# Keeping the keys of a gated recurrence as logarithms: scaled keys straight from the exponential

## The chip, the cores and the metric

The kernel runs on one core of a Trainium2 chip. The metric is the device time of one execution in microseconds (us). Before the change three runs took 2671.22, 2671.25 and 2673.91 us, with a median of 2671.25 us. The engines are PE (matmul; PEld are its weight loads), DVE (vector), ACT (scalar, with the exponential), POOL (GpSimd) and SP (which issues the transfers).

## The reference, cut to what matters

Two layers of an encoder, over 1024 tokens of one new stream and 16 tokens of each of 8 running streams. The first layer's mixer A is a linear recurrence with a decay for each channel, evaluated in blocks:

```
q, fz, i_in, g, p = split(h @ w_in)
log_f = logaddexp(log(lb), log1p(-lb) + log_sigmoid(fz))    # lb is 0 here: log_sigmoid(fz)
k = (1 - lb) * sigmoid(-fz)
q = silu(q) * 128 ** -0.5
b = cumsum(log_f) in the block
scores[t, s] = sum_k q[t,k] * k[s,k] * exp(b[t,k] - b[s,k])     for s <= t
o = scores @ v + (q * exp(b)) @ S
S = exp(b_last) * S + (k * exp(b_last - b)).T @ v
```

After it come an RMS norm for each head, a gate, mixer B (means over the last 2, 4, 8 and 16 tokens with a small product), the output projection, a gated feed-forward net with a convolution, and then a second layer of another kind. The change touches mixer A alone.

## The kernel before, in words

Activations lie with channels on the 128 partitions and tokens on the free axis: 1152 tokens, nine tiles of 128, of which the last holds the samples. `work` has 24 rows of 1152 tokens (its index is called a slot below): 0 to 3 queries, 4 to 7 keys, 8 to 11 values, 12 to 15 gates, 16 to 19 the pooling input, 20 to 23 the running sums b.

**The projection.** `w_in` is applied unit by unit (20 units of 128 output channels, the order is `UNITS`). Every product is three passes, high and low part of weights and input, so a unit is 72 matmuls of 384 columns. ACT makes the high part of a weight piece (`high`), DVE the low part (`low`), POOL multiplies the piece by the norm's gain before that (`scale_weights`), and DVE takes the result out of the banks (`scaled`, `evict`). Units 0 to 8 (`BESIDE = 9`) run alone. In them ACT and DVE turn the forget inputs into log f and keys (`logf_step`, `logf`, `log_keys`, `key_step`), and DVE's scans make b (`decay`, one row of 1152 tokens for each head).

**The attention beside units 9 to 19.** Tile after tile is worked on between the matmuls of a unit (`beside`; `kk` counts its eight parts of nine matmuls). The sample tile p = 0 goes beside units 9 to 12, and tiles p = 1 to 8 beside units 12 to 19. One tile beside its unit is called turn p here. The scores of a tile are the diagonal (`diagonal`) and seven levels (`level`, four for the samples) of block size b = 64 down to 1: within each block of 2b tokens the second half's queries meet the first half's keys, both scaled by exponentials of b minus its value at the middle. A level goes through these steps, each one instruction:

- DVE `diff(m)`: exponents into `ediff`;
- ACT `exponents(m)`: exp of the query half, exp of minus the key half;
- DVE `scale_queries(m)` into `qsc`, POOL `scale_keys(m)` into `ksc`;
- PE `level(m)`: four matmuls; DVE `take(m)`: the masked result into `sct`.

`ediff`, `qsc` and `ksc` have two buffers each. All order is written out by hand: each engine has its own program, and counting semaphores join them. On DVE step q of a turn (q = 1 to 7) does `scale_queries` of level q and `diff` of the level after the next one, on ACT the exponentials of the level after the next one, and on PE `kk` = q - 1 does level q. F is the number of a turn's first level below.

**What else a turn holds.** PE turns the tile's values (`turn_values`, kk 0), its decayed keys (`turn_keys`, kk 5), sums the squares of an earlier tile's outputs (`head_sums`, kk 1, in `spare`), does pooling products, and ends with `outputs` and `state_update` (kk 7). ACT squares those outputs for `head_sums` (`head_square`) at q = 2, takes the root of the sums (`head_root`) at q = 3, and in turns 7 and 8 makes high parts of mixer B's result (`pool_high`); DVE multiplies by the root (`head_norm`) at q = 4 and makes the low parts (`pool_low`).

POOL waits in `scale_keys(m)` until PE has done level m - 2, because `ksc` has two buffers:

```
pool.wait_ge(ek_ready, keys_scaled(m))
if m >= 2:
    pool.wait_ge(level_mm, m - 1)
```

Of the kernel before, what the change touches and what calls it, by code (L numbers as in the profile page):

```python
# [17 lines left out]
F32 = mybir.dt.float32  # L18
# [67 lines left out]
def build(nc, A, O):  # L86
    ctx = ExitStack()
    with ctx:
# [78 lines left out]
        k_scaled = sem("k_scaled")  # L167
# [3 lines left out]
        diag_in = sem("diag_in")  # L171
        kd_diff = sem("kd_diff")
        kd_exp = sem("kd_exp")
        kd_scaled = sem("kd_scaled")
# [138 lines left out]
        resetm = at("resetm", [P, TOK], F32, E0)  # L313
# [3 lines left out]
        vmb = (stt[:, :, :], work[:, 4:8, SEQ:TOK])  # L317
        hstage = work[0:NS * HIST, 4:8, SEQ:TOK]
        poolw = work[:, 20:24, SEQ:TOK]
        prow = (work[:, 8:12, 0:P], work[:, 20:24, 0:P])  # L320
# [5 lines left out]
        ph = at("ph", [P, HEADS, TOK], F32R, slot(20))  # L326
# [316 lines left out]
        HALF = {True: (64, 32, 16, 8, 4, 2, 1), False: (8, 4, 2, 1)}  # L643
# [7 lines left out]
        def keys_scaled(m):  # L651

            return m + 1 - sum(b == 1 for _, b in LEVELS[:m + 1])
# [4 lines left out]
        def eqd(p):  # L658

            return work[:, 8:12, SEQ:TOK] if p else work[:, 20:24, SEQ:TOK]  # L660
# [4 lines left out]
        def pool_part(r):  # L665

            g, c = ((slice(1, 4), tbs(0)), (slice(1, 4), tbs(1)), (slice(0, 1), slice(0, 2 * TB)),
                    (slice(0, 4), tbs(2)))[r]
            return work[:, 16:20, :][:, g, c], ph[:, g, c], pl[:, g, c]
# [328 lines left out]
        def _(pe):  # L998
# [222 lines left out]
            def turn_keys(p):  # L1221
                pe.wait_ge(kd_scaled, p + 1)
# [4 lines left out]
            def diagonal(p):  # L1227
                for h in range(HEADS):
                    mm = pe.matmul(ps[5][:, h * P:(h + 1) * P], work[:, 4 + h, cols(p)], work[:, h, cols(p)],
                                   start=True, stop=True)  # L1230
                mm.then_inc(diag_mm, 1)

            def level(m):
# [3 lines left out]
                if b > 1:  # L1237
                    pe.wait_ge(k_scaled, keys_scaled(m))
                if m >= 2:
                    pe.wait_ge(level_in, m - 1)  # L1240
                for h in range(HEADS):
                    key = ksc[:, m % 2, h, 0:last] if b > 1 else work[:, 4 + h, cols(p)][:, 0:last]
# [54 lines left out]
            def head_sums(i, bank):  # L1297
                pe.wait_ge(osq_ready, i + 1)
                for h in range(HEADS):
                    mm = pe.matmul(ps[bank][:, h * P:(h + 1) * P], ones[:, :], work[:, 4 + h, cols(NORMS[i])],  # L1300
# [3 lines left out]
            def after_samples(kk):  # L1304

                if kk == 0:
                    pe.wait_ge(acc_free, g0 + 24)
                    pe.wait_ge(k_ready, 2)
# [142 lines left out]
            def abo_half(u, n, h, after=None):  # L1451
# [4 lines left out]
                for k in range(4):  # L1456
# [3 lines left out]
                    for c, (w, r) in enumerate(((wh, rh), (wh, rl), (wl, rh))):  # L1460
                        for tb in range(NTB):
                            mm = pe.matmul(ps[3 * u + tb][:, 0:TB], w[:, n % 2, k * P:(k + 1) * P], r[:, k, tbs(tb)],
# [20 lines left out]
            def abo_unit(n, g, sn, sg):  # L1483

                for h, (rh, rl) in enumerate(((oh, ol), (ph, pl))):
                    pe.wait_ge(w_high_ready, n + h + 1)
                    pe.wait_ge(w_low_ready, n + h + 1)
                    for k in range(4):
                        for c, (w, r) in enumerate(((wh, rh), (wh, rl), (wl, rh))):
                            first, last = h == k == c == 0, h == 1 and k == 3 and c == 2  # L1490
                            for tb in range(NTB):
                                if first:
                                    acc_bank(g + tb, sg + tb)
                                mm = pe.matmul(ps[(sg + tb) % BANKS][:, 0:TB], w[:, (sn + h) % 2, k * P:(k + 1) * P],  # L1494
                                               r[:, k, tbs(tb)], start=first, stop=last)
# [7 lines left out]
            def abo_group(d, tb):  # L1503
# [3 lines left out]
                for h, (rh, rl) in enumerate(((oh, ol), (ph, pl))):  # L1507
# [3 lines left out]
                    for k in range(4):  # L1511
                        if tb == 2 and d == 5 and h == 0 and k == 3:
                            norm_block(0, 1, ssq_e)
                        for c, (w, r) in enumerate(((hi, rh), (hi, rl), (lo, rh))):
                            mm = pe.matmul(ps[(g0 + e) % BANKS][:, 0:TB], w[:, k * P:(k + 1) * P],  # L1515
                                           r[:, k, tbs(tb)], start=h == k == c == 0, stop=h == 1 and k == 3 and c == 2)
# [265 lines left out]
        def _(dve):  # L1782
# [13 lines left out]
            def scaled(dst, bank, tb, tick):  # L1796

                dve.wait_ge(pe_tick, tick)
                dve.tensor_tensor(dst, ps[bank % BANKS][:, 0:TB], rstd[:, tbs(tb)], ALU.mult)\
                    .then_inc(acc_free, 1)  # L1800
# [50 lines left out]
            def first_blocks(j, tb, tick):  # L1851
                dve.wait_ge(rms_ready, tb + 1)
                scaled(work[:, UNITS[j], tbs(tb)], 3 * j + tb, tb, tick)
# [9 lines left out]
            def logf(c):  # L1863
                z, f = work[:, 4 + 2 * c:6 + 2 * c, :], work[:, 20 + 2 * c:22 + 2 * c, :]
# [3 lines left out]
            def log_keys(c):  # L1868
                z, f = work[:, 4 + 2 * c:6 + 2 * c, :], work[:, 20 + 2 * c:22 + 2 * c, :]
                dve.wait_ge(logf_ready, c + 1)  # L1870
                dve.tensor_tensor(z, f, z, ALU.subtract).then_inc(logf_ready, 1)

            def decay(h):
                dve.wait_ge(logf_ready, 3 + h // 2)
                dve.wait_ge(reset_ready, 3)
                dve.tensor_tensor_scan(work[:, 20 + h, :], resetm[:, :], work[:, 20 + h, :], 0.0,
                                       ALU.mult, ALU.add).then_inc(decay_ready, 1)

            for j in range(2, BESIDE):
                if j > 2:  # L1880
                    low(2 * j + 1, 2 * j + 1)
                if j == 6:
                    logf(1)
                    log_keys(0)
# [2008 lines left out]
```

## Time and profile before

| | |
|---|---|
| median of three runs | 2671.25 us |
| the profiled execution | 2671.41 us |
| its span | 2669.7 us |
| PE, PEld busy | 2625.6 us (98%), 2555.8 us (96%) |
| DVE busy | 1845.3 us (69%) |
| ACT busy | 937.5 us (35%) |
| POOL busy | 261.6 us (10%) |
| mean granted clock of PE | 0.999 |

The shares are means over stages that differ. The stage of the change lies in the first sixth of the span: units 0 to 8 run until about 131.5 us, the attention stands beside units 9 to 19 until about 406 us, and the output projection follows. A turn is counted here from one tile's diagonal (line 1229) to the next. Times in the rows are microseconds from the span's start. "Matmuls are pipelined": a PE row's length goes on past the moment at which the next may start, so the distance between starts says what PE had to do.

### The profile page before, as it was taken

To read this page: it belongs to the slowest core of one execution; us is meant where nothing else is said; L and a number is where in the kernel's file an instruction comes from. 1 tells how busy PE (TensorE), PEld (TensorE's weight loads), DVE (VectorE), ACT (ScalarE), POOL (GpSimd) and SP (SyncE) were. 2 spreads that over 40 slices of the span, in tenths; PEclk is the share of its full clock that TensorE was granted. 3 is DMA by queue.
4 is the path that set the end of the run, shared out by engine and by line. 5 is a ranking of instruction groups with operands and counts; after the bars stand their busy time and mean duration, and the time that the engine had idled before them with its cause. 6 is when DMAs were issued, how large, how long until landed. Compare 5 with 4: busy or idle time off the path is not lost.

```text
span 2669.7 us, 45385 instructions
## 1 busy us (share of the span) xinstructions
PE 2625.6 (98%) x17820; PEld 2555.8 (96%) x17820; DVE 1845.3 (69%) x3102; ACT 937.5 (35%) x1550; POOL 261.6 (10%) x246
## 2 busy tenths in 40 slices
PE   9999999999999999999999999999999999999998
PEld 8989999999999999999888999999999999999998
DVE  3548985697777779788323755445787777779787
ACT  4414454433232324345322211213533232334344
POOL 3134325100000000000000330001100000000000
PEclk9999999999999999999999999999999999999999
DMA  4111002222222248633111111112222222248533
GB/s 155 40 32 56 24 19 65 97 62 75 75 75 75 75 142 289 232 129 125 39 49 52 47 40 40 43 43 63 91 74 78 74 77 73 78 157 301 204 129 138
DMA packets 236722, 249.01 MB, mean 93 GB/s; under 512 B 13099, under 2 KB 176116, under 8 KB 236276
## 3 DMA queue, kind: packets, MB, share of 16 engines
q1 hardware_dynamic: 236500, 246.36, 28.6%
q8 instruction: 132, 2.16, 0.3%
q14 instruction: 58, 0.48, 0.1%
q10 hardware_dynamic: 32, 0.01, 0.0%
HBM read 202.12 MB, written 44.20 MB: 92 GB/s over the span
## 4 chain that ended last, share of the span: by engine, by line
PE 86%; DVE 8%; issue 2%; ACT 2%; DMA 1%; SPq 0%; DVEq 0%; POOL 0%; ACTq 0%; POOLq 0%
PE banks L1563 34%; PE banks L1644 15%; PE banks L1018 11%; PE banks L1690 7%; PE banks L1043 6%; PE banks L1208 3%; PE banks L1494 1%; PE banks L1068 1%; DMA fraw<-in_w_out_ffn 1%; PE banks L1243 1%; PE banks L1515 1%; PE banks L1146 1%; PE banks L1749 1%; DVE qsc L1917 1%; DVE xs L2253 1%
## 5 line engine op out<-in xcount | busy, mean ns | idle before, releaser
L1563 PE MATMUL banks<-cx,fh 128*128 128x288 f32 x2816 | 486.9, 294 | 1.2 <-issue 0.4
L1563 PEld LDWEIGHTS banks<-cx,fh 128*128 128x128 f32 x2816 | 411.6, 188 | 3.1 <-ACT cw L3317 1.6
L1563 PE MATMUL banks<-cw,fh 128*128 128x288 f32 x2112 | 364.9, 294 | 10.4 <-ACT fh L3306 4.8
L1563 PEld LDWEIGHTS banks<-cw,fh 128*128 128x128 f32 x2112 | 308.6, 188 | 12.5 <-issue 7.7
L1563 PE MATMUL banks<-cx,fl 128*128 128x288 f32 x1408 | 300.0, 294 | 0.0
L1644 PE MATMUL banks<-ysh,fh 128*128 128x288 f32 x1232 | 262.8, 294 | 2.2 <-DVE xs L2465 1.1
L1644 PE MATMUL banks<-ysh,fl 128*128 128x288 f32 x1232 | 262.9, 294 | 0.0
L1644 PE MATMUL banks<-ysl,fh 128*128 128x288 f32 x1232 | 262.3, 294 | 0.0
L3306 ACT ACTIVATE fh<-fraw 128x512 fp32r<-128x512 f32 x220 | 138.4, 631 | 341.7 <-PE banks L1563 289.2
L1563 PE MATMUL banks<-cw,fl 128*128 128x288 f32 x1056 | 225.0, 294 | 0.0
L1563 PEld LDWEIGHTS banks<-cx,fl 128*128 128x128 f32 x1408 | 224.4, 187 | 0.0
L1644 PEld LDWEIGHTS banks<-ysh,fh 128*128 128x128 f32 x1232 | 196.6, 188 | 3.8 <-issue 3.8
L2882 ACT ACTIVATE wh<-raw 128x512 fp32r<-128x512 f32 x104 | 65.5, 630 | 383.9 <-PE banks L1018 213.5
L1644 PEld LDWEIGHTS banks<-ysh,fl 128*128 128x128 f32 x1232 | 196.6, 188 | 0.0
L1644 PEld LDWEIGHTS banks<-ysl,fh 128*128 128x128 f32 x1232 | 196.5, 187 | 0.0
L2249 DVE TENSOR_TENSOR fl<-fraw,fh 128x512 fp32r<-128x512 f32 x220 | 151.5, 691 | 63.9 <-ACT fh L3306 63.8
L1563 PEld LDWEIGHTS banks<-cw,fl 128*128 128x128 f32 x1056 | 168.2, 187 | 0.0
L1806 DVE TENSOR_TENSOR xs<-banks,xs 128x384 f32<-128x384 f32 x192 | 96.5, 550 | 99.9 <-PE banks L1043 46.1
L1786 DVE TENSOR_TENSOR wl<-raw,wh 128x512 fp32r<-128x512 f32 x104 | 85.8, 825 | 111.8 <-ACT wh L2882 111.8
L3372 ACT ACTIVATE fh<-flf 128x512 fp32r<-128x512 f32 x110 | 69.6, 632 | 195.3 <-DVE flf L2428 195.2
L3680 POOL TENSOR_TENSOR raw<-raw,vec 128x512 f32<-128x512 f32 x72 | 84.3, 1176 | 456.9 <-DMA raw<-in_w_uv_c 377.0
L1018 PE MATMUL banks<-xh,wh 128*128 128x384 f32 x552 | 126.3, 336 | 0.0
(434 smaller groups left out, 5177.0 us busy)
## 6 DMA issues: line engine op xcount, KB each, us to landing
fraw<-in_w_out_ffn SPq DMA_DIRECT2D x264, 256.0 KB, 3.4
fraw<-in_w_in_ffn SPq DMA_DIRECT2D x176, 256.0 KB, 4.3
y_scratch<-gate SPq DMA_DIRECT2D x44, 576.0 KB, 3.3
raw<-in_w_uv_c SPq DMA_DIRECT2D x64, 256.0 KB, 2.8
yb<-y_scratch SPq DMA_DIRECT2D x10, 1440.0 KB, 9.1
raw<-in_w_in_ab SPq DMA_DIRECT2D x40, 256.0 KB, 2.9
raw<-in_w_out_c SPq DMA_DIRECT2D x32, 256.0 KB, 2.7
xs<-x_scratch SPq DMA_DIRECT2D x2, 2304.0 KB, 10.2
```

The source lines that it names most:

```text
L1018: mm = pe.matmul(ps[(sg + tb) % BANKS][:, 0:TB], w[:, place, k * P:(k + 1) * P], r[:, kk, tbs(tb)], start=kk == 0 and c == 0, stop=kk == K ...
L1043: mm = pe.matmul(ps[(sg + g0 + tb) % BANKS][:, 0:TB], w[:, place, k * 256 + dd * P:k * 256 + (dd + 1) * P], r[:, k, tbs(tb)], start=k == 0 ...
L1208: mm = pe.matmul(ps[beside_bank(j, tb)][:, 0:TB], w[:, h, k * P:(k + 1) * P], r[:, kk, tbs(tb)], start=first, stop=last)
L1563: mm = pe.matmul(bank[:, M0 + c * CH:M0 + (c + 1) * CH], w[:, pos % RING, k * P:(k + 1) * P], x[:, m, part, c * CH:(c + 1) * CH], start=fi ...
L1644: mm = pe.matmul(psp[f][:, M0 + c * CH:M0 + (c + 1) * CH], w[:, f * P:(f + 1) * P], x[:, r % RINGD, c * CH:(c + 1) * CH], start=kk == 0 an ...
L1690: mm = pe.matmul(ps[g % BANKS][:, :], x[:, k, t * P:(t + 1) * P], w, start=k == 0 and e == 0, stop=k == KD - 1 and e == 2)
L1786: dve.tensor_tensor(wl[:, s % 2, :], raw[:, s % RAWS, :], wh[:, s % 2, :].bitcast(F32), ALU.subtract)\
L1806: dve.tensor_tensor(xs[:, d, tbs(tb)], ps[sg % BANKS][:, 0:TB], xs[:, d, tbs(tb)], ALU.add)\
L2249: dve.tensor_tensor(fl[:, pos % RING, :], src, fh[:, pos % RING, :].bitcast(F32), ALU.subtract)\
L3306: act.activation(fh[:, pos % RING, :], src, ACT.Copy).then_inc(f_high, 1)
L3372: act.activation(hi, src, ACT.Copy).then_inc(f_high, 1)
L3680: pool.tensor_tensor(r, r, g, ALU.mult).then_inc(w_scaled, 1)
```

## The change

Keys are kept as logarithms. `kt` (was slots 4 to 7) first holds the forget input fz; `key_exponents` then makes it b - log k, as fz + b of the token before (a tile's first token keeps fz alone). Three consequences:

- A scaled key is one exponential, exp(mid - (b - log k)). ACT writes it into `ksc` itself (`level_keys`), and POOL's `scale_keys` and `decayed_keys` are gone. `diff` reads the key half from `kt` and the query half from `bt` in one instruction.
- The diagonal needs plain keys: DVE `own_keys(p)` (512 elements a partition) and one exponential for each tile. They are placed in `ksc` as the keys of level b = 1, which is now first in each tile.
- ACT's `level_keys(m)` has the wait for PE's level m - 2 that POOL had.

`kt` and the sums `bt` (was slots 20 to 23) lie tile by tile, so that the scans are five (`scanned`: four of 1024 elements, one of 512) where there were four of 1152.

```
-        HALF = {True: (64, 32, 16, 8, 4, 2, 1), False: (8, 4, 2, 1)}
+        HALF = {True: (1, 64, 32, 16, 8, 4, 2), False: (1, 8, 4, 2)}
...
             def turn_keys(p):
-                pe.wait_ge(kd_scaled, p + 1)
+                pe.wait_ge(kd_exp, p + 1)
...
             def diagonal(p):
+                pe.wait_ge(ek_ready, FIRST[p] + 1)
                 for h in range(HEADS):
-                    mm = pe.matmul(ps[5][:, h * P:(h + 1) * P], work[:, 4 + h, cols(p)], work[:, h, cols(p)],
+                    mm = pe.matmul(ps[5][:, h * P:(h + 1) * P], ksc[:, FIRST[p] % 2, h, :], work[:, h, cols(p)],
...
+            def key_exponents(r):
+
+                dve.wait_ge(decay_ready, r + 1)
+                c = P if r < 4 else SL
+                z, b = (scanned(t, r).rearrange("p (n c) -> p n c", c=c) for t in (kt, bt))
+                dve.tensor_tensor(z[:, :, 1:], z[:, :, 1:], b[:, :, 0:c - 1], ALU.add).then_inc(k_ready, 1)
...
+            def own_keys(p):
+
+                m = FIRST[p]
+                if m >= 2:
+                    dve.wait_ge(level_mm, m - 1)
+                dve.tensor_tensor(ksc[:, m % 2], kt[:, TILES[p]], bt[:, TILES[p]], ALU.subtract).then_inc(own_diff, 1)
...
-            dve.wait_ge(decay_ready, HEADS)
+            decay(4)
+            key_exponents(3)
+            key_exponents(4)
+            dve.wait_ge(k_ready, 5)
             dve.wait_ge(q_act, 2)
             dve.wait_ge(setup_done, 3)
             diff(0)
+            own_keys(0)
             diff(1)
...
-            def key_step(c):
-                z = work[:, 4 + 2 * c:6 + 2 * c, :]
-                act.wait_ge(logf_ready, 3 + c)
-                act.activation(z, z, ACT.Exp).then_inc(k_ready, 1)
-
...
+            def level_queries(m):
+
+                p, b = LEVELS[m]
+                ev = blocks(ediff[:, m % 2], 2 * b)[:, :, :, b:]
+                act.wait_ge(diff_ready, m + 1)
+                act.activation(ev, ev, ACT.Exp).then_inc(eq_ready, 1)
+
+            def level_keys(m):
+
+                p, b = LEVELS[m]
+                if b == 1:
+                    act.wait_ge(own_diff, p + 1)
+                    act.activation(ksc[:, m % 2], ksc[:, m % 2], ACT.Exp, scale=-1.0).then_inc(ek_ready, 1)
+                    return
+                if m >= 2:
+                    act.wait_ge(level_mm, m - 1)
+                    if LEVELS[m - 2][1] == 1:
+                        act.wait_ge(diag_mm, LEVELS[m - 2][0] + 1)
+                act.activation(blocks(ksc[:, m % 2], 2 * b)[:, :, :, 0:b],
+                               blocks(ediff[:, m % 2], 2 * b)[:, :, :, 0:b], ACT.Exp, scale=-1.0).then_inc(ek_ready, 1)
...
-            def scale_keys(m):
...
-            def decayed_keys(p):
-                pool.wait_ge(kd_exp, p + 1)
-                pool.tensor_tensor(ekd[:, :, :], ekd[:, :, :], work[:, 4:8, cols(p)], ALU.mult).then_inc(kd_scaled, 1)
```

Below is DVE's order where the attention begins, from the end of unit 8 to the first level. `scaled` is the row `work<-banks,rstd`, the scans are the rows with `resetm`, and `ediff`, `ksc` and `qsc` are the tiles named above. Before:

```order
L1786 TENSOR_TENSOR wl<-raw,wh 128x512
L1876 SCALAR_TENSOR_TENSOR work<-resetm,work 128x1152
L1786 TENSOR_TENSOR wl<-raw,wh 128x512
L1799 TENSOR_TENSOR work<-banks,rstd 128x384 x3
L1910 TENSOR_TENSOR ediff<-work 128x512 x2
L1917 TENSOR_TENSOR qsc<-work,ediff 128x256
```

And now:

```order
L1802 TENSOR_TENSOR wl<-raw,wh 128x512
L1818 TENSOR_TENSOR work<-banks,rstd 128x384 x3
L1896 SCALAR_TENSOR_TENSOR kb<-resetm,kb 128x1024
L1903 TENSOR_TENSOR kb<-kb 128x8x127
L1896 SCALAR_TENSOR_TENSOR kb<-resetm,kb 128x512
L1903 TENSOR_TENSOR kb<-kb 128x8x127
L1903 TENSOR_TENSOR kb<-kb 128x32x15
L1935 TENSOR_TENSOR ediff<-kb 128x256
L1948 TENSOR_TENSOR ksc<-kb 128x512
L1940 TENSOR_TENSOR ediff<-kb 128x512
L1955 TENSOR_TENSOR qsc<-work,ediff 128x256
```

Two scans and three key exponents that had no counterpart between unit 8's last block and the first exponents stand there now, and `own_keys` behind the first exponents.

Next is ACT's order from q = 1 to q = 3 of turn 2, with what each row waits for. `ediff` rows are the exponentials, `wh` is `high`, `work<-banks` or `kb<-banks,vec` are `outputs` and `head_root`, `vtok` is `values`, `spad` is `own_rows`. The row `work<-work` or `kb<-work` that waits for `o_out` is `head_square`. Before:

```order
L3022 ACTIVATE ediff<-ediff 128x16x16 [waits diff_ready]
L3024 ACTIVATE ediff<-ediff 128x16x16
L2882 ACTIVATE wh<-raw 128x512 [waits pe_tick,w_scaled]
L3088 ACTIVATE work<-banks 128x4x128 [waits o_mm]
L3022 ACTIVATE ediff<-ediff 128x32x8 [waits diff_ready]
L3024 ACTIVATE ediff<-ediff 128x32x8
L3096 ACTIVATE work<-work 128x4x128 [waits o_out]
L3044 ACTIVATE vtok<-banks 128x512 [waits sd_mm,v_mm]
L3136 ACTIVATE spad<-work 128x8x16 [waits states_stored,acc_free]
L3022 ACTIVATE ediff<-ediff 128x64x4 [waits diff_ready]
L3024 ACTIVATE ediff<-ediff 128x64x4
L3101 ACTIVATE work<-banks,vec 128x4x128 [waits onorm_mm]
```

And now:

```order
L3056 ACTIVATE ediff<-ediff 128x8x32 [waits diff_ready]
L2925 ACTIVATE wh<-raw 128x512 [waits pe_tick,w_scaled]
L3138 ACTIVATE work<-banks 128x4x128 [waits o_mm]
L3069 ACTIVATE ksc<-ediff 128x8x32 [waits diag_mm,level_mm]
L3056 ACTIVATE ediff<-ediff 128x16x16 [waits diff_ready]
L3069 ACTIVATE ksc<-ediff 128x16x16 [waits level_mm]
L3146 ACTIVATE kb<-work 128x512 [waits o_out]
L3094 ACTIVATE vtok<-banks 128x512 [waits sd_mm,v_mm]
L3186 ACTIVATE spad<-work 128x8x16 [waits states_stored,acc_free]
L3056 ACTIVATE ediff<-ediff 128x32x8 [waits diff_ready]
L3069 ACTIVATE ksc<-ediff 128x32x8 [waits level_mm]
L3151 ACTIVATE kb<-banks,vec 128x512 [waits onorm_mm]
```

The rows that write the scaled keys wait for `level_mm` now, and `outputs` has moved ahead of the first of them; `head_square` stands behind the second.

## Rows read from the trace of the kernel before

**Rows 1.** Windows, turns 3, 4, 6: length; busy PE, PEld, DVE, ACT, POOL; clock, DMA.

```profile
246.18:273.25 27.07, 24.65 (x178) 23.46 (x178) 24.50 (x39) 11.45 (x31) 11.50 (x9) 1.00 0.07 21
273.25:301.17 27.92, 26.42 (x184) 24.66 (x184) 25.82 (x43) 12.88 (x34) 10.10 (x9) 1.00 0.07 20
...
328.21:354.95 26.74, 26.74 (x191) 25.55 (x191) 23.44 (x40) 14.26 (x34) 8.60 (x9) 1.00 0.12 31
```

**Rows 2.** Waits of PE from 131 to 410 us: total us, times, longest.

```profile
PE banks L1243 <- DVE qsc L1917: 5.4, 7, 1.3
PE banks L1255 <- DVE sct L1938: 1.6, 2, 1.3
```

**Rows 3.** Waits of POOL from 125 to 405 us.

```profile
POOL ksc L3733 <- PE banks L1243: 99.6, 35, 8.1
```

**Rows 4.** Timeline, turn 4: start, length, engine, line; DVE beside POOL and alone.

```profile
275.87 1.22 POOL L3680 TENSOR_TENSOR raw<-raw,vec 128x512 f32<-128x512 f32 x1
276.30 1.34 DVE L1910 TENSOR_TENSOR ediff<-work 128x512 f32<-128x512 f32 x1
...
280.27 0.69 DVE L1910 TENSOR_TENSOR ediff<-work 128x512 f32<-128x512 f32 x1
```

**Rows 5.** Timeline of DVE, end of unit 8 to the first exponents.

```profile
123.35 2.55 DVE L1876 TENSOR_TENSOR_SCAN work<-resetm,work 128x1152 f32<-128x1152 f32 x1
...
126.21 0.69 DVE L1786 TENSOR_TENSOR wl<-raw,wh 128x512 fp32r<-128x512 f32 x1 [0.31 <-ACT wh L2882]
131.38 1.49 DVE L1799 TENSOR_TENSOR work<-banks,rstd 128x384 f32<-128x384 f32 x3 [4.48 <-PE banks L1018]
```

**Rows 6.** Groups of DVE by shape: busy us, mean ns.

```profile
L2008 DVE TENSOR_TENSOR sums<-work 128x1023 f32<-128x1023 f32 x4 | 4.8, 1210 | 0.0
```

**Rows 7.** Timeline of PE and ACT where the attention begins.

```profile
133.78 1.05 PE L1229 MATMUL banks<-work 128*128 128x128 f32 x8
135.45 1.02 PE L1243 MATMUL banks<-qsc,ksc 128*120 128x64 f32 x8 [0.62 <-POOL ksc L3733]
136.29 0.77 PE L1208 MATMUL banks<-xh,wh 128*128 128x384 f32 x3
```

**Rows 8.** Windows of PE: length, busy time, granted clock.

```profile
160.70:164.00 3.30, 3.30 (x10) 0.50 0.00 0
530.00:540.00 10.00, 6.72 (x49) 1.00 0.00 1
```

**Rows 9.** Timeline, turn 4: head squares, second level, head sums, head root, head norm.

```profile
272.83 0.61 ACT L3096 ACTIVATE work<-work 128x512 f32<-128x512 f32 x1
...
276.62 0.81 PE L1243 MATMUL banks<-qsc,ksc 128*96 128x64 f32 x8
...
277.27 1.11 PE L1300 MATMUL banks<-work,ones 128*128 128x128 f32 x8
...
278.42 0.69 ACT L3101 ACTIVATE work<-banks,vec 128x512 f32<-128x512 f32 x1
```

**Rows 10.** Groups of ACT by shape: key exponentials of 256 elements.

```profile
L3024 ACT ACTIVATE ediff<-ediff 128x256 f32<-128x256 f32 x51 | 20.7, 405 | 0.0
```

**Rows 11.** Timeline, turn 7 and turn 8 around `pool_high` and `pool_low`.

```profile
361.50 0.91 PE L1243 MATMUL banks<-qsc,ksc 128*112 128x64 f32 x8
361.92 1.15 ACT L3150 ACTIVATE ph<-work 128x1152 fp32r<-128x1152 f32 x1
363.10 1.42 DVE L2039 TENSOR_TENSOR pl<-work,ph 128x1152 fp32r<-128x1152 f32 x1 [1.60 <-ACT ph L3150]
364.91 1.05 PE L1243 MATMUL banks<-qsc,ksc 128*120 128x64 f32 x8 [0.88 <-DVE qsc L1917]
...
389.84 0.91 PE L1243 MATMUL banks<-qsc,ksc 128*112 128x64 f32 x8
...
391.12 1.34 DVE L2039 TENSOR_TENSOR pl<-work,ph 128x768 fp32r<-128x768 f32 x1 [3.15 <-ACT ph L3150]
392.84 1.05 PE L1243 MATMUL banks<-qsc,ksc 128*120 128x64 f32 x8 [0.47 <-DVE qsc L1917]
```

More of the change, by code:

```diff
@@ L649, in cols, with exponents_of @@
             return slice(TILES[p] * P, (TILES[p] + 1) * P)
-        def keys_scaled(m):
-            return m + 1 - sum(b == 1 for _, b in LEVELS[:m + 1])
+        def exponents_of(p, b):
+            lower = kt[:, TILES[p]]
+            row = [list(lower.ap[0]), [2 * b, HEADS * P // (2 * b)], [16 * TOK + b, 2], [1, b]]
+            return bass.AP(lower.tensor, lower.offset, row)
         def blocks(ap, b):
@@ L658, in eqd @@
         def eqd(p):
[L660 removed]
+            return work[:, 8:12, SEQ:TOK] if p else bt[:, NT - 1]
         SIDES = (slice(0, SEQ - P), slice(SEQ, TOK))
@@ L668, in pool_part, with scanned, pair, tokens @@
                     (slice(0, 4), tbs(2)))[r]
-            return work[:, 16:20, :][:, g, c], ph[:, g, c], pl[:, g, c]
+            y, lo = (t[:, g, c].rearrange("p g (t c) -> p g t c", c=P) for t in (work[:, 16:20, :], pl))
+            return y, ph[:, g, c.start // P:c.stop // P, :], lo
+        def scanned(t, r):
+            return t[:, 2 * r:min(2 * r + 2, NT)].rearrange("p t h c -> p (t h c)")
+        def pair(t, c):
+            return t[:, :, 2 * c:2 * c + 2, :].rearrange("p t h c -> p t (h c)")
+        def tokens(r, k, tb):
+            return r[:, k, 3 * tb:3 * tb + 3, :] if r is ph else r[:, k, tbs(tb)]
         def past(p):
@@ L1241, in level @@
                 for h in range(HEADS):
-                    key = ksc[:, m % 2, h, 0:last] if b > 1 else work[:, 4 + h, cols(p)][:, 0:last]
+                    key = ksc[:, m % 2, h, 0:last]
                     mm = pe.matmul(ps[6 + m % 2][0:last, h * 64:(h + 1) * 64], key, qsc[:, m % 2, h, :],
@@ L1494, in abo_unit @@
                                 mm = pe.matmul(ps[(sg + tb) % BANKS][:, 0:TB], w[:, (sn + h) % 2, k * P:(k + 1) * P],
-                                               r[:, k, tbs(tb)], start=first, stop=last)
+                                               tokens(r, k, tb), start=first, stop=last)
                                 if last:
@@ L3164, in _ @@
             for q in range(1, 5):
-                exponents(q + 1)
+                if q == 4:
+                    level_keys(FIRST[1])
+                level_queries(q + 1)
+                if q != 3:
+                    level_keys(q + 1)
                 if q == 3:
@@ L3764, in _ @@
                 gain = V_MIX if p < 8 else None
-                for q in range(1, 8):
-                    scale_keys(FIRST[p] + q - 1)
-                    if q == 6:
-                        decayed_keys(p)
-                    if q in (3, 6):
-                        scale_weights(2 * j + (2 if q == 3 else 3), 0, 4, gain)
-                    if p == 1 and q == 2:
-                        decay_samples(3)
+                if p == 1:
+                    decay_samples(3)
+                for s in (2, 3):
+                    scale_weights(2 * j + s, 0, 4, gain)
             scale_weights(42, 0, 4, None)
```

164 lines of the change are left out of this document (77 added, 87 removed).

## The prediction, made before the changed kernel ran

> **What bounds the kernel now.** I read the windows of the stage first. A turn lasts 26.7 to 28.4 us from turn 3 to turn 7. In turn 6 PE is busy for all of its 26.74 us, while in turns 3 and 4 it idles 2.4 and 1.5 us beside a DVE that is busy for 24.5 and 25.8 us [rows 1]. So PE's own work sets the end almost everywhere, and DVE where mixer B's sums stand beside the levels. The waits agree: PE waited 5.4 us for scaled queries and 1.6 us for the last `take`, 7.0 in all [rows 2]. POOL's own wait was long and free: 99.6 us for PE's levels in 35 times [rows 3]. It is POOL's `scale_keys` that wait there, and on POOL nothing urgent stands behind them.
>
> Next I looked at what makes DVE so busy. The same subtraction of 512 elements takes 0.69 us alone and 1.34 us beside POOL [rows 4]. POOL is busy 11.5 and 10.1 us in turns 3 and 4 [rows 1].
>
> Then the two places that the change's order touches: the beginning of the attention [rows 5, 7], and ACT from q = 2 on [rows 9, 11].
>
> **The start: two scans and three key exponents come in front of the first level.** Before, all scans were done when DVE ended unit 8's last block at 131.38 + 1.49 = 132.9 us, and it had idled 4.48 us before that block [rows 5]. Now `decay(3)` and everything after it stand behind the block, so that this idle time hides nothing. A scan of 1152 elements takes 2.55 us [rows 5], by elements 2.27 for 1024 and 1.13 for 512. A key exponent is like the addition of 1023 elements, 1.21 us [rows 6], twice, and some 0.6 for 480. The sum is 2.27 + 1.21 + 1.13 + 1.21 + 0.6 = 6.4, and about 6.3 since starts overlap a little. Then `diff(0)` (256 elements, 0.4), `own_keys(0)` (0.6), ACT's exponential of 512 elements (0.6, as the 0.61 of [rows 9]) and two hand-overs of 0.1. The diagonal starts at 132.8 + 6.3 + 1.8 = 140.9 us where it started at 133.78, because it needed no exponent before. The first level follows at 141.7 where it stood at 135.45 after a wait of 0.62 on POOL [rows 7]. The next unit part (136.29 before) is late by **6.3 us**. The bounds are 5.5 (the small ones at no cost of their own) and 7.5 (POOL's gain multiply at DVE's side, 0.65 as in [rows 4]). Nothing gives it back soon, since PE is full until turn 1 ends.
>
> **The clock.** PE stands still for 7.1 us there. The longest idle stretches of this kind in the trace, two within 530 to 540 us that make up its missing 3.3 us, left the clock at 1.00. From 160.7 to 164 us it was 0.50, the 1.2 GHz level, after small matmuls of 16 columns, and those 3.3 us did half of the work: 1.7 us lost [rows 8]. No row shows an idle time of 7 us, so the bounds are 0 and twice the row, 3.4. I take **1.7**, the row. The Trainium skill, "TensorE: Matmul & The Clock Gate", section "Why this matters for your kernels", warns that an idle gap between bursts of matmuls brings the clock back to the half rate; by it this term is there and not nothing, and the waits of turns 7 and 8 below would bring it again. By the row alone it could be absent.
>
> **ACT takes over POOL's wait, with other work behind it.** `level_keys(m)` waits for PE's level m - 2. On ACT the next instructions queue behind it, above all at q = 2: `level_keys(F+3)` waits for PE's second level F+1, and `head_square` stands behind it. But PE wants the squares for `head_sums` immediately after level F+1. In turn 4 the squares began at 272.83, four microseconds before that level at 276.62, and `head_sums` followed at 277.27 with no wait [rows 9]. Now: the level ends at 276.62 + 0.81 = 277.43, the key exponential takes 0.40 [rows 10], the squares 0.61 [rows 9], with 0.1 for overlap and hand-over. PE starts at 278.5, 1.2 us late. This is in each of turns 2 to 8: 7 x 1.2 = **8.4 us**. The bounds are 0.9 and 1.4 for each.
>
> At q = 3 `level_keys(F+4)` waits for the third level, and `head_root`, the exponential of the queries and, in turns 7 and 8, `pool_high` stand behind it; DVE's `pool_low` waits for that in front of the next `scale_queries`. In turn 7 the third level ends at 361.50 + 0.91 = 362.41. Behind it now come 0.40, the root's 0.69 and 0.61, the queries' 0.61, less 0.2 of overlap, and `pool_high`'s 1.15: it ends at 365.7 where it ended at 363.07 [rows 11]. Level F+3, at 364.91 with a wait of 0.88, is 2.6 us later. In turn 8 the same sum from 389.84 + 0.91 = 390.75 gives an end of 393.7 for 391.1, and `pool_low` needs 0.9 in place of its 1.34 with POOL gone [rows 11]: 2.2 us. Together **4.8 us**, between 3 and 6. In turns 2 to 6 the same delay makes DVE's `head_norm` wait for about a microsecond, for which DVE has room now.
>
> **What POOL's absence gives.** POOL keeps two gain multiplies of 1.22 us a turn [rows 4], 2.4 of its 10.1 to 11.5. If DVE loses 0.4 us for each us of POOL, as 0.65 in 1.34 suggests with some of them meeting no one, DVE gains some 3 us a turn and pays 0.6 for `own_keys`. From 25.8 busy in turn 4 that is 23.4, below PE's pace. So PE's waits on DVE go, but not all 7.0: the 0.88 and 0.47 of turns 7 and 8 hang on `pool_high` [rows 11], and about 0.5 of the 1.6 stays because `own_keys` stands in front of the last `take`. I take **-5 us**, with bounds of 0 and -9 (PE's rows run on past their ends, so short waits are hidden; turn 4 is 1.2 us longer than turn 6, which has one more head sum of 0.75, and only 1.5 of it shows as idle).
>
> **Edits at little or nothing.** ACT's two long key exponentials of before unit 8 go, and ACT waited there. ACT pays 0.2 us more at level 1, for whole keys, and is busy for half of a turn. In turns 4 to 7 `keys(p)` comes behind `level_keys` and is 0.2 late for `outputs`. In turn 1 `key_decay`, `values` and `high` now come behind the fifth level, which makes the last level some 0.3 late. Together **+1.2 us**, 0 to 2.5. The new layout changes strides only. If a strided read did cost something, it would be DVE's two-region `diff`, and DVE has room.
>
> **The sum.** 6.3 + 1.7 + 8.4 + 4.8 - 5.0 + 1.2 = 17.4 us, on the profiled execution's 2671.41: **2688.8 us**. The median of the runs is 0.16 below that execution, so that no correction is needed. What follows the mixer (output projection, nets, second layer) has the same order and shifts as a whole.
>
> **Rivals.**
>
> *DVE's relief decides (not slower), 0.12.* If ACT gets through its queue in time (the squares done before level F+1 ends), the 8.4 and the 4.8 fall away, the clock holds, and all 9 us of DVE-made delay return: 6.3 - 9 = -2.7, **2668.7 us**. For it speaks that DVE is the busiest follower of PE and is slowed to double by POOL. Against it stands the order: the squares come behind an instruction that can't start before that level ends. It decides from the point where the relief is over the 6.3 us of the start.
>
> *The clock falls at each long wait, 0.13.* At the start for as long as two such stretches (3.4 us), and after the waits of about 3 us in turns 7 and 8 (1.7 each): 17.4 + 1.7 + 3.4 = 22.5, **2693.9 us**. The rule of the Trainium skill named above would make it so; the row of 530 to 540 us, with shorter gaps, speaks against it [rows 8].
>
> *Contention isn't what slows DVE, 0.06.* The change then takes POOL's work away without the gain: 17.4 + 5, **2693.8 us**. Against it: the same instruction is seen both ways in one turn [rows 4].
>
> *The forecast, 0.69.* Its own range from the bounds, not all at one end, is 2682 to 2694 us.
>
> **How the numbers follow.** A measurement of this kernel can tell about 0.2%, 5.3 us, from no change. The forecast and the second and third rivals are slower by more, with 0.88 of the chance; I leave 0.04 of it to an error of the working that is large enough to end within 0.2%. The first rival ends within 0.2% in most of its range, a third of it faster. So slower 0.84, same 0.11, faster 0.05. The range that holds 8 in 10 reaches down toward the first rival, to 2674, and up to 2696.
>
> **What would show it.** In the changed profile: the diagonal of the samples at about 141 us with PE waiting 7 us for ACT's `ksc`; a granted clock of 0.5 behind it, or not; in each of turns 2 to 8 a wait of PE's `head_sums` on ACT's squares of about 1.2 us; `pool_low` waiting for ACT over 3 us in turns 7 and 8; DVE's `diff` at a mean near 0.7 us instead of the two lengths; POOL near 2.4 us a turn. Turn 6 should become longer (28.4 us), turn 3 should not. The prediction is wrong if `head_sums` starts on time, or if the turns from 2 to 8 together are not longer than before: I expect about 9 us more.

## The result, and where the profile after shows it

The changed kernel takes **2691.59 us** (median of 6 runs, 2686.88 to 2694.60) against 2671.70 us (6 runs, 2670.88 to 2673.91) on the same chip: **1.0073, 95% interval 1.0060 to 1.0086**, slower. The prediction said 2688.8.

The waits of PE from 125 to 430 us, then those of ACT and DVE that stand behind them (total us, times, longest):

```profile
PE banks L1317 <- ACT kb L3146: 7.8, 7, 1.1
PE banks L1260 <- DVE qsc L1955: 7.2, 4, 3.4
PE banks L1247 <- ACT ksc L3063: 6.9, 1, 6.9
PE banks L1247 <- DVE stt L1997: 1.5, 3, 1.0
```

```profile
ACT ksc L3069 <- PE banks L1260: 81.1, 35, 5.3
DVE pl L2074 <- ACT pht L3200: 13.9, 3, 7.0
```

In the kernel before PE waited 9.1 us here, 7.0 of them in the two groups of [rows 2]. Now it waits 24.4, of which 20.8 are in three places: once for the first keys (6.9), seven times for the squares of the head sums (line 1317, 7.8), and in turns 7 and 8 for queries (3.4 and 2.7). POOL's harmless 99.6 us [rows 3] have become 81.1 us of ACT, with work queued behind them.

Windows of turns 3, 4, 6, 7 and 8, against [rows 1] (length; busy PE, PEld, DVE, ACT, POOL; clock):

```profile
256.26:282.22 25.96, 24.56 (x178) 23.35 (x178) 20.68 (x40) 12.18 (x31) 2.08 (x2) 1.00 0.08 23
282.22:310.07 27.85, 26.45 (x184) 24.64 (x184) 22.72 (x44) 13.72 (x34) 2.08 (x2) 1.00 0.07 18
338.14:366.25 28.11, 26.99 (x191) 25.49 (x191) 20.18 (x41) 14.68 (x34) 1.04 (x1) 1.00 0.11 30
366.25:399.96 33.71, 29.17 (x184) 27.00 (x183) 20.51 (x39) 15.24 (x33) 0.00 (x0) 0.90 0.06 17
399.96:427.96 28.00, 23.74 (x165) 22.86 (x163) 16.34 (x29) 17.11 (x31) 1.06 (x1) 0.94 0.03 10
```

Turn 3 is 1.1 us shorter than before although it holds a wait of 1.1 us for the squares: DVE is busy for 20.7 in place of 24.5 us. Turn 6 is 1.4 us longer; turns 7 and 8 lose most, and their clock column is below 1.

The start, on PE, against [rows 7]:

```profile
141.04 2.04 PE L1247 MATMUL banks<-work,ksc 128*128 128x128 f32 x8 [6.91 <-ACT ksc L3063]
```

Turn 7, against [rows 11]:

```profile
374.04 0.81 PE L1260 MATMUL banks<-qsc,ksc 128*96 128x64 f32 x8
374.89 0.42 ACT L3069 ACTIVATE ksc<-ediff 128x256 f32<-128x256 f32 x1 [2.74 <-PE banks L1260]
375.22 0.67 ACT L3151 ACTIVATE kb<-banks,vec 128x512 f32<-128x512 f32 x1
...
376.98 1.15 ACT L3200 ACTIVATE pht<-work 128x1152 fp32r<-128x1152 f32 x1
378.15 1.36 DVE L2074 TENSOR_TENSOR pl<-work,pht 128x1152 fp32r<-128x1152 f32 x1 [5.78 <-ACT pht L3200]
379.43 0.42 DVE L1955 TENSOR_TENSOR qsc<-work,ediff 128x256 f32<-128x256 f32 x1
```

ACT stands 2.74 us for a level before it makes keys; `pool_high`, DVE's `pool_low` and the queries that PE wants at 379.90 follow one another behind that.

PE by windows (length, busy, granted clock):

```profile
137.50:141.00 3.50, 0.00 (x0) 0.50 0.00 0
141.00:147.00 6.00, 5.96 (x24) 0.50 0.15 44
160.70:164.00 3.30, 3.28 (x19) 1.00 0.21 59
380.00:386.00 6.00, 6.00 (x21) 0.50 0.00 0
414.00:416.50 2.50, 2.50 (x9) 0.50 0.03 7
```

The clock falls to 0.50, the 1.2 GHz level, during the first wait and at the stalls of turns 7 and 8. It stays there for 10.3, 7.0 and 3.5 us. The kernel before had only the fall at 160.7 in this stage [rows 8], and that one is absent here.

### The profile page after: what moved, and what is told of

The parts are those of the page before. It is cut to its first block, busy times and chain, and to the rows that moved or that the text cites. A ratio compares the mean times of both kernels' runs of the same rounds, so it can differ in the third digit from the quotient of the medians.

```text
span 2692.8 us, 45311 instructions
## 1 busy us (share of the span) xinstructions
PE 2631.5 (98%) x17820; PEld 2561.2 (95%) x17820; DVE 1821.3 (68%) x3115; ACT 938.5 (35%) x1556; POOL 195.6 (7%) x186
## 4 chain that ended last, share of the span: by engine, by line
PE 88%; DVE 7%; issue 2%; ACT 2%; DMA 1%; SPq 0%; DVEq 0%; POOL 0%; ACTq 0%
PE banks L1579 34%; PE banks L1660 15%; PE banks L1035 10%; PE banks L1706 7%; PE banks L1060 6%; PE banks L1225 4%; PE banks L1260 2%; PE banks L1510 1%; PE banks L1085 1%; DMA fraw<-in_w_out_ffn 1%; PE banks L1531 1%; PE banks L1163 1%; PE banks L1765 1%; DVE xs L2296 1%; PE banks L1478 0%
## 5 line engine op out<-in xcount | busy, mean ns | idle before, releaser
L1579 PE MATMUL banks<-cw,fh 128*128 128x288 f32 x2112 | 364.9, 294 | 10.4 <-ACT fh L3365 4.8
L2925 ACT ACTIVATE wh<-raw 128x512 fp32r<-128x512 f32 x104 | 65.5, 629 | 389.3 <-PE banks L1035 209.2
L1035 PE MATMUL banks<-xl,wh 128*128 128x384 f32 x552 | 125.3, 334 | 0.0
```

The lines of the kernel that those rows point to most:

```text
L1035: mm = pe.matmul(ps[(sg + tb) % BANKS][:, 0:TB], w[:, place, k * P:(k + 1) * P], r[:, kk, tbs(tb)], start=kk == 0 and c == 0, stop=kk == K ...
L1579: mm = pe.matmul(bank[:, M0 + c * CH:M0 + (c + 1) * CH], w[:, pos % RING, k * P:(k + 1) * P], x[:, m, part, c * CH:(c + 1) * CH], start=fi ...
L2925: act.activation(wh[:, s % 2, :], raw[:, s % RAWS, :], ACT.Copy).then_inc(w_high_ready, 1)
```

## The experiments

Times are medians, and each ratio is to the kernel before, run beside: 2671.41 us for the first four experiments, 2672.36 for the three after them. The first three edits move one thing each in the changed kernel. The code is cut to what matters, with `...` where lines are left out.

**Squares first.** The only edit is in step 2 of turns 2 to 8 on ACT.

```diff
+                    if p >= 2 and q == 2:
+                        head_square(p - 2 if p < 7 else p - 1)
                     if m + 2 < len(LEVELS) and (p, q) != (1, 1) and q != 6:
                         level_keys(m + 2)
...
-                            head_square(p - 2 if p < 7 else p - 1)
```

> In step 2 of turns 2 to 8 ScalarE squares the heads' outputs before it makes the next level's keys; nothing else moves. Theory (the head sums wait because ScalarE waits for TensorE before the keys, seven waits of 1.1 us, 7.8 us in all in the changed kernel): the waits of the head sums fall below 0.2 us each and the time falls by 7 to 8 us, to about 2684. Rival (TensorE would wait in these turns anyway, since VectorE or the keys that now come 0.6 us later decide): the waits move to the levels and the time stays within 2 us of 2691.6.

Measured: 2683.06 us, 1.0044 (1.0030 to 1.0058), 8.5 us below the changed kernel, a little more than expected. The head sums no longer appear among PE's waits, which now begin:

```profile
PE banks L1260 <- DVE qsc L1955: 7.2, 4, 3.4
PE banks L1247 <- ACT ksc L3063: 6.9, 1, 6.9
```

Each of turns 2 to 6 is 1.1 to 1.3 us shorter (turn 3: 24.84 us). So the seven waits had lengthened the turns by their full size, and the keys, made 0.6 us later, keep nobody waiting. The rival falls.

**`pool_high` first.** In step 3 of turns 7 and 8.

```diff
+                    if p >= 7 and q == 3:
+                        pool_high(2 * (p - 7))
                     if m + 2 < len(LEVELS) and (p, q) != (1, 1) and q != 6:
                         level_keys(m + 2)
...
-                        if p == 7 and q in (3, 6):
-                            pool_high(q // 3 - 1)
-                        if p == 8 and q == 3:
-                            pool_high(2)
+                        if p == 7 and q == 6:
+                            pool_high(1)
```

> In step 3 of turns 7 and 8 ScalarE makes pool_high before the keys for which it waits 2.7 us. Theory (VectorE's pool_low, and the scaled queries behind it, come late because of that wait, and TensorE's clock falls for 6.5 and 3.7 us behind each stall): the stalls of 3.4 and 2.7 us go and the clock stays at 1.00; turn 7 takes 29 instead of 33.7 us, turn 8 25 instead of 28.0, in all -7 to -9 us, about 2683.5. If only the stalls went and the low clock stayed, it would be -5 to -6. Rival (the two turns end where VectorE ends its own 24 us of work): 0 to -2 us.

Measured: 2682.36 us, 1.0038 (1.0024 to 1.0052), down by 9.2, where 7 to 9 were expected. Its windows of turns 7 and 8:

```profile
367.27:394.39 27.12, 26.00 (x185) 24.50 (x184) 20.63 (x39) 15.05 (x33) 0.00 (x0) 1.00 0.07 21
394.39:417.85 23.46, 21.90 (x166) 21.34 (x164) 16.41 (x29) 16.81 (x31) 1.06 (x1) 1.00 0.04 12
```

Turn 7 is shorter by 6.6 and turn 8 by 4.5 us. The waits that went are 3.42 and 2.71, so the falls of the clock that went with them are worth 3.2 and 1.8, or 5.0 us on stalls of 6.1. These figures are from the changed kernel's first profile, the slowest of its runs. By its second profile (below), with turns of 32.31 and 27.98 us and the same stalls, the falls are worth 1.8 and 1.8, and the two turns lose 9.7 us, nearer to the 9.2 of the medians.

**Scans early.** DVE waits for PE's blocks inside unit 8; the scans go there, and what only later turns need goes behind the first levels.

```diff
+                if j == 8:
+                    decay(2)
+                    decay(3)
                 low(2 * j + 2, 2 * j + 2)
+                if j == 8:
+                    decay(4)
+                    key_exponents(4)
...
-            dve.wait_ge(k_ready, 5)
+            dve.wait_ge(k_ready, 2)
...
+                if q == 3:
+                    for r in range(1, 4):
+                        key_exponents(r)
```

> The scans of pairs 3 and 4 and the sample keys are made inside unit 8, where VectorE waits for its matmuls, and the key exponents of tiles 2 to 7 after the first levels. Theory (the first diagonal waits 6.9 us for VectorE's chain of scans): the diagonal starts at 135 instead of 141.0, TensorE waits about 1 us there, its clock stays at 1.00, and everything behind comes 7 to 9 us earlier: about 2683.5. Rival A (ScalarE's table load and exponentials hold the diagonal): diagonal at 137 or later, -4 us at most. Rival B (the time comes back before turn 1, because the three key exponents of 3.5 us stand in front of the levels of the samples): turn 1 starts less than 3 us earlier.

Measured: 2684.71 us, 1.0046 (1.0032 to 1.0060), down by 6.9, where 7 to 9 were expected. PE's first diagonal, and the windows from there to turn 1:

```profile
135.18 1.13 PE L1247 MATMUL banks<-work,ksc 128*128 128x128 f32 x8 [0.67 <-ACT ksc L3068]
```

```profile
135.18:199.08 63.90, 63.00 (x377) 57.51 (x378) 33.17 (x53) 12.03 (x27) 13.70 (x10) 1.00 0.12 34
```

In the changed kernel the same stretch is the row

```profile
141.04:207.92 66.88, 65.99 (x376) 60.49 (x377) 29.88 (x50) 12.01 (x27) 13.70 (x10) 0.95 0.11 32
```

Turn 1 starts 8.84 us earlier: 5.86 of them because the first diagonal is earlier, 2.98 because the stretch behind it has no low clock. Neither rival holds. The whole 8.8 doesn't reach the median (6.9 do); why is not shown. This edit leaves turns 7 and 8 alone, and the profile has their falls of the clock still.

**All three together.**

> The edits of the three kernels before this one together. Theory (three places, independent of each other, make up all of the loss, and VectorE's relief is a gain on top): the sum of the three, -21 to -25 us against the changed kernel, 2667 to 2671, so 0.9985 of the kernel before. Rival (they share cover: once the waits are gone the turns end with VectorE and ScalarE): -10 to -15 us, 2677 to 2682.

Measured: **2665.80 us (11 runs), 0.9981 (0.9972 to 0.9990)**: faster than before, and 25.8 us below the changed kernel, where 21 to 25 were expected and the three single savings add up to 24.6. Within the noise none of them is lost beside the others, and the rival falls. Windows of turns 3, 6, 7 and 8:

```profile
246.73:271.56 24.83, 24.62 (x179) 23.36 (x179) 20.67 (x40) 12.20 (x31) 2.08 (x2) 1.00 0.08 23
324.90:351.83 26.93, 26.93 (x190) 25.47 (x191) 20.18 (x41) 14.68 (x34) 1.04 (x1) 1.00 0.11 31
351.83:377.79 25.96, 25.96 (x184) 24.50 (x183) 20.53 (x39) 15.05 (x33) 0.00 (x0) 1.00 0.07 21
377.79:400.10 22.31, 21.87 (x166) 21.34 (x164) 16.42 (x29) 16.81 (x31) 1.06 (x1) 1.00 0.04 13
```

PE is idle for 0.2 us at most in turns 3, 6 and 7, and for 0.4 in turn 8. Against [rows 1] turn 3 is 2.2 us shorter. From turn 2 to the output projection it is 178.06 us where before took 186.01: this is what the change gives once its waits are out of the way. Up to 1.4 us of it may belong to the earlier `pool_high` alone, since the kernel before also waited 0.88 and 0.47 us there [rows 11]; the kernel before with such moves was not run.

**The clock kept busy through the wait.** The changed kernel, with matmuls whose results nothing reads:

```diff
                     pe.wait_ge(acc_free, g0 + 24)
+                    for _ in range(36):
+                        pe.matmul(ps[6][:, 0:TB], wh[:, 0, 0:P], xh[:, 0, tbs(0)], start=True, stop=True)
                     pe.wait_ge(q_act, 2)
```

> The changed kernel, with 36 matmuls of 384 columns, whose results nothing reads, in TensorE's wait ahead of the first diagonal; the wait itself (the diagonal at 141.0) is left as it is. Theory (TensorE's clock falls because it has nothing to do for 6.9 us, and that low clock from 137 to 147 costs 3.0 us of the 8.9 us that the start loses): the clock reads 1.00 from 134 to 148, the first diagonal still starts at 141, the diagonal of turn 1 comes 63.9 us behind it instead of 66.9, and the time falls by 3 us to about 2688.6. Rival (the clock falls in this stretch whatever TensorE does, or the time comes back in a later wait): the stretch stays at 66.9 us and the time at 2691.6.

Measured: 2689.64 us, 1.0063 (1.0050 to 1.0077), 2 us down and not to be told apart from the changed kernel by the intervals. PE by windows:

```profile
134.50:141.50 7.00, 6.93 (x40) 1.00 0.00 0
142.09:149.00 6.91, 6.91 (x49) 1.00 0.16 40
167.00:173.00 6.00, 6.00 (x19) 0.50 0.01 3
```

Half of the theory holds: with PE at work the clock stays at 1.00 from 134 to 149, so the fall there was made by the idleness. All four profiles that have the 6.9 us wait unfilled show a fall that begins in it, at 137.1 to 138.7 us, and none of the nine others shows one there. The Trainium skill, "TensorE: Matmul & The Clock Gate", section "Why this matters for your kernels", warns of such gaps, and these rows agree. But the clock fell at 166.8 instead, for 7 us in the middle of steady work, and the stretch took 66.40 us, not 63.9. By the stretch it is nearly the rival's 66.9; the time lies between the two, 2.0 us down and 2.7 by the ratios. So the saving isn't shown, and keeping the clock is not the same as having no wait. The fall at 166.8 belongs to a kind that comes without a wait, taken up below.

**POOL made busy again**, on the kernel with the three edits, in turns 2 to 4:

```diff
+                if 2 <= p <= 4:
+                    pool.wait_ge(states_stored, 16 * HEADS)
+                    for q in range(7):
+                        n = 512 if q == 4 else 256
+                        if q != 4:
+                            pool.wait_ge(eq_ready, FIRST[p] + q + 1)
+                        linked(pool.tensor_tensor(sin_[:, 0, 0:n], sin_[:, 0, 512:512 + n], sin_[:, 0, 512:512 + n], ALU.mult))
```

> The kernel with the three edits, and in turns 2 to 4 GpSimd does seven multiplications per turn (six of 128x256, one of 128x512) on memory that nobody reads, at the moments when it scaled the keys in the kernel before. Theory (GpSimd's work makes VectorE's instructions beside it longer, and the change took this away: the kernel with the three edits needs 24.69, 24.83 and 26.65 us for these turns, that before 25.49, 27.07 and 27.92): VectorE's busy time rises by 2.5 to 4 us per turn to what it was before (24.5 in turn 3), single instructions of 0.69 us read 1.3 or more, and the three turns take 2 to 4 us longer in all: 2668 to 2670. Rival (VectorE's relief came from its shorter list of instructions, and turns 3 and 4 got shorter because the keys' way over GpSimd is gone): VectorE's busy time rises by less than 1 us per turn and the time stays at 2665.8.

Measured: 2672.18 us (11 runs), 1.0001 (0.9992 to 1.0010): 6.4 us up, or 5.3 by the two ratios, more than the 2 to 4 expected. The three turns together take 82.07 in place of 76.17 us. The windows of turns 2, 3, 4:

```profile
222.74:248.57 25.83, 24.86 (x182) 23.76 (x182) 20.14 (x39) 12.55 (x32) 8.64 (x9) 1.00 0.07 20
248.57:275.85 27.28, 24.76 (x178) 23.37 (x179) 23.42 (x40) 12.19 (x31) 9.99 (x9) 1.00 0.07 21
275.85:304.81 28.96, 26.94 (x185) 24.55 (x185) 25.40 (x44) 13.62 (x34) 8.36 (x7) 1.00 0.07 19
```

DVE executes the same 40 instructions in turn 3, in 23.42 us for 20.67, and the turn takes 27.28 us, about what it took in the kernel before. (Turn 4, with 28.96, takes 1.0 more than before: the added work is like POOL's old work, not a copy of it.) One place in turn 4 where it is seen:

```profile
290.80 2.55 POOL L3745 TENSOR_TENSOR raw<-raw,vec 128x512 f32<-128x512 f32 x2
...
291.25 1.19 DVE L1802 TENSOR_TENSOR wl<-raw,wh 128x512 fp32r<-128x512 f32 x1
292.37 2.06 DVE L2053 TENSOR_TENSOR sums<-sums 128x1024 f32<-128x1024 f32 x1
```

The rival falls: DVE's list is the same in both, so the relief is contention that is gone. Two groups of DVE in turns 2 to 4 (busy us, mean ns), first with the three edits, then with POOL made busy:

```profile
L1944 DVE TENSOR_TENSOR ediff<-kb 128x512 f32<-128x512 f32 x18 | 12.4, 691 | 1.9 <-DVE qsc L1959 0.5
L2053 DVE TENSOR_TENSOR sums<-sums 128x1024 f32<-128x1024 f32 x5 | 6.6, 1319 | 0.0
```

```profile
L1944 DVE TENSOR_TENSOR ediff<-kb 128x512 f32<-128x512 f32 x18 | 14.0, 776 | 1.9 <-DVE qsc L1959 0.5
L2053 DVE TENSOR_TENSOR sums<-sums 128x1024 f32<-128x1024 f32 x5 | 8.1, 1618 | 0.0
```

The groups of DVE in turns 2 to 8 of the kernels before and after show the same, over more instructions:

```profile
L1910 DVE TENSOR_TENSOR ediff<-work 128x512 f32<-128x512 f32 x38 | 32.7, 859 | 4.3 <-DVE qsc L1917 0.5
L1917 DVE TENSOR_TENSOR qsc<-work,ediff 128x256 f32<-128x256 f32 x47 | 27.9, 593 | 0.0
L1799 DVE TENSOR_TENSOR work<-banks,rstd 128x384 f32<-128x384 f32 x21 | 10.3, 548 | 0.0
```

```profile
L1940 DVE TENSOR_TENSOR ediff<-kb 128x512 f32<-128x512 f32 x39 | 27.0, 691 | 3.8 <-DVE qsc L1955 0.5
L1955 DVE TENSOR_TENSOR qsc<-work,ediff 128x256 f32<-128x256 f32 x47 | 20.1, 427 | 0.0
L1818 DVE TENSOR_TENSOR work<-banks,rstd 128x384 f32<-128x384 f32 x21 | 10.4, 548 | 0.0
```

The two that read both operands from SBUF, the on-chip memory of the tiles, get 0.17 us shorter on the mean. The one that reads an accumulator bank in PSUM (`banks`) and one SBUF operand stays at 548 ns, and it has 549 and 548 ns without and with POOL's work in the experiment too. The Trainium skill, "SBUF — State Buffer", section "Who interferes with whom", has this as a rule: a DVE instruction with two SBUF inputs contends with a GpSimd instruction that reads SBUF. These rows agree.

**State first**, two further moves on the kernel with the three edits (below: the kernel with five moves):

```diff
+                    if q == 2 and p > 1:
+                        next_state(p - 1)
                     scale_queries(m)
+                    if q == 7 and p == 1:
+                        low(2 * j + 2, 2 * j + 2)
```

The state stood further back in DVE's order before, and the split of weights (`low`) stood in front of the last queries of turn 1; now it stands behind them.

> The kernel with the three edits, and two more moves on VectorE: in step 2 of turns 2 to 8 the new state is made before the level's queries and exponents, and at the end of turn 1 the split of weights comes behind the last queries. Theory (the last waits of TensorE are for VectorE's place in line: 0.96, 0.26 and 0.24 us for the state in turns 2, 5 and 6, and 0.93 us for the queries at the end of turn 1): these waits go and the time falls by 1.5 to 2.4 us, to about 2664. Rival (the queries of the level behind it come 1.1 us later and TensorE waits for those instead): no change.

Measured: **2664.34 us, 0.9966 (0.9954 to 0.9978)**, the best of all. From the diagonal of turn 1 to the output projection it takes 197.4 us, where the kernel with the three edits took 200.6: 3.2 us less, more than the 2.4 expected. Turn 2's diagonal with three edits, and with five:

```profile
222.04 1.16 PE L1247 MATMUL banks<-work,ksc 128*128 128x128 f32 x8 [0.96 <-DVE stt L2001]
```

```profile
223.85 1.06 PE L1247 MATMUL banks<-work,ksc 128*128 128x128 f32 x8
```

The wait for the state is gone. In the medians 1.5 us shows, by the ratios 4.0, and the intervals of the two ratios overlap, so the size of the gain is open. The profile has a fall of the clock at 161 us that the profile of the three edits lacks.

**Second profiles of unchanged programs**, for this fall.

> The program with the five moves once more, unchanged, for a second profile. In its first profile the clock read 0.50 from about 161 to 167.5, and the stretch from the first diagonal to that of turn 1 took 66.4 us; the kernel with three moves, the same up to there, took 63.9 us without a low clock. Theory (this fall of the clock comes in some executions and not in others, by nothing in the program): the second profile has 63.9 us, or 65 to 66.5 with a fall in another place or of another length. Rival (the program's order decides): 161 to 167.5 and 66.4 us again.

> The changed kernel once more, unchanged, for a second profile. Theory (the clock falls at the long wait ahead of the first diagonal and at the stalls of turns 7 and 8 in most executions, but where exactly it returns differs, so its times spread over 8 us): the waits are 6.9, 3.4 and 2.7 us again, the clock reads 0.50 behind the first wait, and the two stretches behind the stalls differ in length by up to 2 us from the first profile. Rival (the falls at turns 7 and 8 were chance): no low clock there.

> The program with three moves once more, unchanged, for a second profile. In its first one the clock never fell and the stretch from the first diagonal to that of turn 1 took 63.9 us. Theory A (the fall at about 161 us comes by chance): either outcome; with a fall the stretch is 65 to 66.5 us. Theory B (the order of the program decides, since the program with five moves fell at 161 us twice): no fall, 63.9 us.

> The kernel before once more, unchanged, for a second profile. In its first one the clock fell from 160.7 to 164 us and the stretch from the first diagonal to that of turn 1 took 65.4 us. Theory A (chance): another place, another length or no fall, 63.9 to 66.5 us. Theory B (the program decides): 160.7 to 164 and 65.4 us again.

Measured: 2664.26, 2690.39, 2665.50 and 2672.76 us. With five moves the clock fell at about 161 us both times, for the same 66.4 us to turn 1, so taken alone these two look like the rival (the program decides). The kernel before repeated its fall (65.5 us). With the three edits there was no fall in the first profile and one in the second, with 64.84 in place of 63.93 us to turn 1, so there theory B fails. The rows of the three edits in both profiles:

```profile
161.50:164.50 3.00, 3.00 (x16) 1.00 0.00 0
```

```profile
161.50:164.50 3.00, 3.00 (x9) 0.50 0.00 0
```

PE is busy in both; the same 3 us hold 16 matmuls at the one clock and 9 at the other. Six profiles settle the question further, for PE has the same instructions up to turn 1 in all of them, and the other engines too: scans early, three edits twice, POOL made busy, five moves twice. From the first diagonal to turn 1 they took 63.90, 63.93, 64.84, 64.79, 66.38 and 66.41 us, with no fall in the first two, one of 3.5 us in the next two and one of 7 us in the last two. So the order of the program does not decide it, neither for the three edits nor for the five moves. What does, with no wait ahead of the fall, stays open.

The shorter fall shows what such a fall costs. PE comes 1.6 us late out of it, and 0.7 of that returns at this row, which has a wait only where the clock didn't fall:

```profile
168.19 1.10 PE L1298 MATMUL banks<-stt,kdt 128*128 128x512 f32 x2 [0.44 <-DVE stt L2011]
```

The changed kernel's second profile had the waits of 6.9, 3.4 and 2.7 us again and the falls behind them again: 6.9 us at the low clock for 10.3 at the first wait, 3.5 for 7.0 in turn 7, 3.5 in turn 8. It had one more, of 3.5 us at 168.8. Its turn 7 took 32.31 in place of 33.71 us. So the falls behind the waits come again, as the theory had it, and their length differs.

## Why the prediction was right, and where its terms were off

The changed kernel's profiled execution reaches the output projection 21.26 us later than the one before (427.96 for 406.70). By the prediction's own terms:

| term | predicted | measured, and from what |
|---|---|---|
| start, without clock | +6.3 | +6.6: diagonal 7.26 later, less the 0.62 on POOL [rows 7] |
| clock | +1.7 | +7.1: 2.98, 3.2 and 1.8 at the three waits, less 0.9 for the fall of before that is absent |
| head sums | +8.4 | +7.8, seven waits |
| `pool_high` | +4.8 | +4.8: 3.42 + 2.71, less 0.88 and 0.47 of before [rows 11] |
| POOL's absence | -5.0 | -6.1, what is left of turns 2 to 8 |
| small ones | +1.2 | +1.05, turn 1 |
| sum | 17.4 | 21.3 |

The mechanism was right at the three large places (start, head sums, `pool_high`), and an edit at each, which takes the wait away, gave its time back: 6.9, 8.5 and 9.2 us. The term that was mis-sized is the clock, 1.7 for 7.1 us. The prediction took one fall, priced by the only row it had, and put the case of three falls (2693.9) at 0.13 as a rival. By its clock the profiled execution, 2694.60, was that rival. The second profile, at 2690.39, has the same three falls, two of them shorter, and a fourth. The median, 2691.6, lies between forecast and rival. The row of 530 to 540 us, which spoke against falls in short gaps, holds gaps of 1.5 and 1.8 us and was no guide for stalls of 2.7 and 3.4. The prediction's reading of the fall at 160.7 us as 1.7 us lost fits what PE loses in it (1.6 in the second profile of the three edits), but 0.7 came back at a later wait. In turn 8 the same 3.5 us cost 1.8.

Three smaller points. The term of small ones has the right size by luck. It was put down mainly to ACT; what turn 1 shows is PE waiting at its end for DVE's queries and state, 0.93 and 0.97 us, where it waited 0.77 and 0.21 before, and the two moves of the last kernel on DVE took turn 1 from 22.55 to 21.10 us. DVE's relief was larger than reckoned: turns 3, 4 and 6 have it busy for 3.8, 3.1 and 3.3 us less, not some 2.4. And the 7.0 us that the prediction gives as PE's waits in all are the two largest groups out of 9.1 us.

The profiled execution's remaining 1.8 us of span are not the change's. They are two waits of PE in the feed-forward nets of the two layers, at 1103 and 2499 us, for DVE's `xs<-xs,banks`: 1.47 and 1.42 us, where the kernel before had 0.61 and 0.52. Unchanged programs move as much there: in the second profiles the two waits add up to 0.8 us after and 2.0 before.

The rival on DVE's relief had a real force in it: -6.1 us, and 8 once the waits are gone. But its condition, squares done before level F+1 ends, was not met in any of seven turns. The kernel with the three edits ends near its 2668.7, at 2665.8, but by another sum, since the start's 6.3 us, which this rival kept, are largely gone there too. The rival that contention isn't what slows DVE is refuted by the kernel with POOL made busy.

## What to carry to other kernels

When a waiting instruction moves from an engine with nothing behind it to one with a queue, the cost is not its duration but what is queued behind the wait; first look whether the urgent instruction can stand ahead of it. Taking work off GpSimd paid on VectorE, though GpSimd was hardly waited for (0.6 us), and it reached the end where VectorE was what TensorE waited for. A stall of TensorE should be priced with the low clock that may stand behind it: the stalls of 2.7, 3.4 and 6.9 us cost 1.4 to 1.9 times their length here. And one profile is one execution: two of the same program differed by 1.4 us in a single turn.

## What the runs showed of the hardware that was not expected

The clock fell to 0.50 during a wait of 6.9 us in all four profiles that have it unfilled, and at the stalls of 3.4 and 2.7 us in all five profiles that have these, and stayed there for 3.5 to 10.3 us. It also fell in steady work: at about 161 us in 6 of 13 profiles, in one of the three-edit program and not in the other, and at 166.8 to 169.4 us in three more. In the four profiles with the first wait the time at the low clock between 137 and 173 us came to 10.3 to 10.4 us each time, in one fall (two profiles) or in two, and the stretch to turn 1 took 66.8 to 67.1 us. Filling the first wait with matmuls kept the clock up there and was followed by a fall 25 us later. GpSimd's additional 6 to 8 us of multiplications per turn made VectorE's same instructions 2.1 to 2.8 us longer.
